# Identity products on TensorE ahead of the waits of three kinds of attention in a float32 model of one core

## The reference

```
first block: q, k normed, 8 query heads, 2 key heads, width 64
  s = q k' / 8 over the block itself, the one before it and 16 meta tokens, masked
  p = softmax([s, sink]);  out = p v                  # 5 blocks of 128, beside s5_ssm(...)
mixer A: score = sum_h w_h relu(iq_h ik');  keep the best 256 keys
         p = softmax(q k' / 8 + bias, kept keys only);  out = p v     # 4 heads of 64
mixer D: p = softmax(q k' / sqrt(96), causal);          out = p v     # 4 heads, keys of 96
```

## Time and profile before

| | |
|---|---|
| median of three runs | 4370.68 us |
| profiled execution | 4363.53 us |
| its span | 4362.3 us |
| TensorE busy | 4140.0 us, 19325 records |
| VectorE busy | 2287.6 us |
| ScalarE busy | 1407.6 us |
| mean granted clock | 0.956 |

### The profile page before, as it was taken

The page is one execution under the profiler, slowest core; times in us unless marked ns, Lnnn a source line. Parts: engine busy times, 40 slices in busy tenths (PEclk is TensorE's granted clock), DMA queues, the critical chain, the costliest instruction groups (busy, mean ns, idle before and its releaser), DMA issues.

```text
span 4362.3 us, 47791 instructions
## 1 busy us (share of the span) xinstructions
PE 4140.0 (95%) x19325; PEld 3249.6 (74%) x19325; DVE 2287.6 (52%) x3714; ACT 1407.6 (32%) x2385; POOL 192.0 (4%) x350
## 2 busy tenths in 40 slices
PE   8889999999999999999999978999999999789999
PEld 7767887666678888888878765787878787557877
DVE  5748887777734444444333776433243248754331
ACT  3444322333333333333222432422232233333221
POOL 8400000000000000000000010000000000100000
PEclk9779999999999999999999987999999999779999
DMA  3012444555566666662332210233323322003332
GB/s 114 11 39 86 125 138 127 182 185 178 175 195 197 190 188 189 189 189 85 93 96 73 82 46 1 78 92 97 97 78 96 97 73 78 27 1 97 92 97 73
DMA packets 253340, 473.59 MB, mean 109 GB/s; under 512 B 15856, under 2 KB 138896, under 8 KB 250944
## 3 DMA queue, kind: packets, MB, share of 16 engines
q1 hardware_dynamic: 253024, 470.45, 35.4%
q10 hardware_dynamic: 96, 0.08, 0.0%
HBM read 399.96 MB, written 70.52 MB: 108 GB/s over the span
## 4 chain that ended last, share of the span: by engine, by line
PE 79%; DVE 9%; ACT 3%; issue 1%; DMA 0%; POOL 0%; DVEq 0%; ACTq 0%; POOLq 0%; SPq 0%
PE ps L354 24%; PE ps L356 24%; PE ps L355 24%; DVE arena L2048 2%; PE ps L536 1%; DVE arena L2937 1%; DVE st L2935 1%; DVE arena L2044 1%; DVE arena L2045 1%; PE ps L1897 1%; PE ps L2425 1%; PE ps L2397 1%; ACT arena L1945 1%; DVE wlast L345 1%; PE ps L2400 1%
## 5 line engine op out<-in xcount | busy, mean ns | idle before, releaser
L345 DVE TENSOR_TENSOR wlast<-wraw,wlast 128x1024 fp32r<-128x1024 f32 x406 | 495.8, 1225 | 764.5 <-ACT wlast L335 764.2
L354 PE MATMUL ps<-XH,wlast 128*128 128x512 f32 (+1 forms) x1904 | 785.6, 413 | 0.0
L356 PE MATMUL ps<-XH,wlast 128*128 128x512 f32 (+1 forms) x1904 | 753.7, 396 | 0.0
L355 PE MATMUL ps<-XL,wlast 128*128 128x512 f32 (+1 forms) x1904 | 752.7, 395 | 0.0
L335 ACT ACTIVATE wlast<-wraw 128x1024 fp32r<-128x1024 f32 x406 | 426.8, 1056 | 407.6 <-PE ps L356 388.1
L345 DVE TENSOR_TENSOR wtwo<-wraw,wtwo 128x1024 fp32r<-128x1024 f32 x212 | 261.1, 1232 | 444.3 <-ACT wtwo L335 443.8
L356 PEld LDWEIGHTS ps<-XH,wlast 128*128 128x128 f32 x1904 | 360.3, 189 | 87.4
L354 PEld LDWEIGHTS ps<-XH,wlast 128*128 128x128 f32 x1904 | 361.3, 190 | 76.0 <-issue 5.0
L355 PEld LDWEIGHTS ps<-XL,wlast 128*128 128x128 f32 x1904 | 361.7, 190 | 70.9
L354 PE MATMUL ps<-XH,wtwo 128*128 128x512 f32 (+1 forms) x944 | 387.3, 410 | 0.0
L355 PE MATMUL ps<-XL,wtwo 128*128 128x512 f32 (+1 forms) x944 | 372.0, 394 | 0.0
(11 more groups left out here) (476 smaller groups left out, 6825.7 us busy)
## 6 DMA issues: line engine op xcount, KB each, us to landing
wraw<-in_ut SPq DMA_DIRECT2D x128, 512.0 KB, 4.2
wraw<-in_v SPq DMA_DIRECT2D x128, 512.0 KB, 3.9
wraw<-in_ffn_gate SPq DMA_DIRECT2D x88, 512.0 KB, 3.5
wraw<-in_ffn_up SPq DMA_DIRECT2D x88, 512.0 KB, 3.5
wraw<-in_ffn_down SPq DMA_DIRECT2D x88, 512.0 KB, 3.5
acts<-arena SPq DMA_DIRECT2D x128, 256.0 KB, 4.5
gates<-arena SPq DMA_DIRECT2D x16, 2048.0 KB, 9.0
arena<-gates SPq DMA_DIRECT2D x32, 1024.0 KB, 8.2
```

What stands on the lines that cost most here:

```text
L345: ve.e.tensor_tensor(W.items[n][8], W.rawof(n), W.items[n][7], ALU.subtract).then_inc(*ve.up("wlo", n))
L354: mm(out, lh, rh, start=start, stop=False)
L355: mm(out, lh, rl, start=False, stop=False)
L356: return mm(out, ll, rh, start=False, stop=stop)
```

## The change

A helper `busy(o, n)` is added to `Kernel`. It issues n matmuls of the 128 by 128 identity with itself, float32, into the first 128 columns of a bank, with start and stop set; the result is overwritten later or never read. It is called at three places:

- in `turn` of the first block's attention, 8 for head 0 and 2 for each other head. `open` has moved ahead of the wait for `se`, and the identity products stand between them;
- in its `value`, 2 for each head, in columns 256 to 383 of the result's bank, ahead of the wait for `PT`;
- in `turn` of the mixers' attentions, 3 for each head, between `open` and the wait for `ex`.

```diff
+    def busy(self, o, n):
+        for _ in range(n):
+            self.pe.e.matmul(o[:, 0:128], self.ident[:, :], self.ident[:, :], start=True, stop=True)
...
             def turn(hq):
+                o = k.open(3, 4, "pT", n, hq)
+                k.busy(o, 2 if hq else 8)
                 pe.wait_ge(*at("se", n))
-                o = k.open(3, 4, "pT", n, hq)
                 for kb in self.blocks(i):
...
             def value(h):
                 pv = k.open(4, 5, "pv", n) if h == 0 else k.got("pv", n)
+                k.busy(pv[:, 256:384], 2)
                 pe.wait_ge(*at("PT", n, h))
...
         def turn(n, h):
             o = k.open(b + 2, b + 3, id, "t", n, h)
+            k.busy(o, 3)
             pe.wait_ge(*at("ex", id, n, h))
```

## The result

The changed kernel takes 4388.16 us, the median of six runs (4387.67 to 4394.58). The kernel before took 4375.09 us beside it (six runs, 4369.83 to 4382.39). The ratio is 1.0032 with a 95% interval of [1.0019, 1.0045]: slower by a third of a per cent. Its profiled execution took 4388.0 us with a span of 4386.8 us, which is 24.5 us more than the span before. The mean granted clock rose from 0.956 to 0.968. So the clock did what the identity products were to do, and the kernel still lost. (The kernel before spread over 30 us in 80 runs, with a median of 4368.3 us; against that one the change costs 20 us.)

What follows compares the result with a forecast made beforehand. TensorE, VectorE, then TensorE were taken to bound the first attention; VectorE's search, then TensorE, each mixer. 4363.5 us + 19 (first attention) + 12 (two mixers) gave 4394.5, and 7.2 to the median gave 4402 us, range 4358 to 4435.

Steps and rivals of the forecast that it cites:

- The products fill no wait: At the attentions' transposes: products come after the bank's wait, fill next to nothing, and can pay only through the clock.
- 0.22 us a product at full clock: Price of one identity product on TensorE: 0.22 us at full clock, 0.43 at half; all 368 are 81 or 158 us.
- First attention to 153 us, +9.6: From 112 us, where TensorE sets the pace: 54 products, first 8 at half clock, 3.9 us gained; net +9.6 us.
- 153 to 199.4 us, +3: First attention's middle stretch, where VectorE sets the pace: 66 products, 14.5 us, mostly covered by VectorE's long products; +3 us.
- 199.4 to 246 us, +6.8: First attention's last stretch, where TensorE sets the pace: 56 products, 9.7 us gained from the clock; net +6.8 us.
- VectorE's search in the mixer: Each mixer to 2673 us: VectorE's search for the best keys fills 73.2 of 79 us and leads the chain.
- A mixer to 2673 us, +1: Mixer's first part: 45 products, 10 to 19 us, with VectorE as cover; +1 us, ends -3 and +3.
- A mixer's second part, +5: From 2673 to 2738 us: 51 products, nothing to hide under; +5 us, between +4.3 if the clock returns early and +13.7.
- The offset to the median, 7.2 us: Whole kernel: the profiled execution lies 7.2 us under the median of the runs, so 4394.5 us became 4402.
- The first rival: Full clock throughout: products hold the clock full in both attention stages, kernel faster by 10 us, 4361 us; chance 0.12.
- No response of the clock: Rival: half-clock stretches stay; +47 us for the first attention, +33 for the mixers, 4451 us; chance 0.10.
- hidden products: Rival: TensorE's idle time in the first attention's three stretches and the clock gain take the products up, 4371 us; chance 0.10.

Runs made afterwards that it cites:

- e7_double: The changed kernel with every count of identity products doubled (16, 4, 4 and 6; 736 in all); 4444.09 us, ratio 1.0174.
- e3_thin: The changed kernel with its 368 products using only 32 rows of the identity instead of 128, same columns; 4583.1 us, ratio 1.0527.
- e5_eight_only: The changed kernel with only the 8 products ahead of head 0 in the first attention kept, 64 in all; 4359.4 us, ratio 0.9982.
- e8_select: The kernel before plus 98 products at selected places in the first block and ahead of each mixer's first state product, score banks opened early; 4350.29 us, ratio 0.9958.
- e9_state_only: The kernel before plus only 20 identity products ahead of part B's first state product in each mixer, 40 in all; 4353.87 us, ratio 0.9982.

## Why the prediction was right

The direction held, and 4388 us lie inside the range around 4402. The size held less well: I had +31 us, and it is +13 us by the medians beside each other, +20 against all runs of the kernel before, and +24.5 in the profiles. The steps, one by one:

- *The products fill no wait.* Right. Transposes wait for nothing behind them, the bank's waits stand ahead of the products, and doubling the products costs 37 of 38.7 us (`e7_double`).
- *0.22 us a product at full clock.* Right: 1.79 us for eight. Nearly all 352 records of the first attention run at full clock.
- *First attention to 153 us, +9.6.* Right: +9.4 at that instruction on TensorE, +7.1 on VectorE. Only the first eight products at half, as assumed, and here they took 2.6 us instead of 3.4, since the clock returned among them.
- *153 to 199.4 us, +3.* Too small. On TensorE it is +7.4, for 14.5 us of products. VectorE's own steps in it are only 2.4 us later, so its long products did cover them, until 215 us; then it waited 8.95 us for TensorE where it had waited 1.91, and the offset was +17.7 at 206 us. The cover put the loss off and did not take it up. (My 3.8 us for the clock were 3.1: TensorE was busy 6.2 us at half clock there.)
- *199.4 to 246 us, +6.8.* Too large. On TensorE it is -0.9: the clock rose to 0.93, over the 0.75 that I had named, and gave back the whole price of 56 products. That the sum of the attention came out near (+16.1 for +19) is luck: these two terms were wrong in opposite ways by 4.4 and 7.7 us.
- *VectorE's search in the mixer.* I read 73.2 us as the search. That is all of VectorE's busy time in the stretch; lines 2935 and 2937 are 14.5 and 14.4 us of it. The term that hung on it, VectorE as the cover, came out near all the same.
- *A mixer to 2673 us, +1.* +2.1 and +1.4.
- *A mixer's second part, +5.* Too large: +1.5 and +1.6. The offset falls by 5.3 us at 2699, since the clock is back at 2693.8 us, where before, shifted by 15.7 us, it would have been 2712.5; then it rises by 6.8 to 2739 with the products at full clock. So the dense products did bring the clock back before the long scores, which is the nearer of my two ends (+4.3) and a bit beyond it. All four mixers that have these products show such a fall, by 4.7 to 5.3 us; so do two of the six without any product.
- *Between the mixers' stretches.* Not in my sum: another +2.5 us behind the first mixer's attentions and +0.7 behind the second's. The clock falls there at other times than before. `e5_eight_only`, without a product in the mixers, has +2.7 behind the first one as well, so I can't call these effects of the change. From 2390 us to the end the offset rises by 10.3 us, for a forecast of +12.
- *The offset to the median, 7.2 us.* This step failed. I took the distance of one profiled execution of the kernel before from the median of three runs and added it. After has 4388.0 in its profile and 4388.16 as its median. The 7.2 us were the chance place of one execution in a spread of 30 us. Without this term the sum says 4394.5. In the profiles the change costs +24.5, for +31 in my sum.
- *The first rival's price.* TensorE is busy 61 of 65 us in a mixer's second part, so full clock would give back 11.0 us there and not 11.7. The rival is 1 or 2 us dearer by that, which changes nothing.

The rivals: full clock throughout got its clock (1.00 and 0.93 in the last two stretches of the first attention, 0.96 in the mixer's second part), but the price of the products is larger than the clock returned; I had this rival at -10 us and the change is at +13 by the medians. Its ends for the attention were +2.4, 0 and -5.2, and TensorE's are +9.4, +7.4 and -0.9. No response of the clock is ruled out by `e3_thin` beside the change, and hidden products by `e7_double` and by the offsets of +16.1 and +14.7 behind the first attention.

What the Trainium skill advises (TensorE: Matmul & The Clock Gate, "Why this matters for your kernels"), to keep TensorE busy so that its clock stays up, held where the products were dense in rows, and the clock did stay up. It did not hold for the thin products, where TensorE was busy 106.2 of 108.5 us at 0.50. And a clock that stays up was not a faster kernel: the 176 products of the first attention bought it for 16 us.

Open: what decides where the clock falls. It is down from 111 to 152 us in `e8_select` and `e9_state_only` and only until 140 or 141 us in the two profiles of the kernel before, with the same TensorE work ahead. Whether less than 20 products, or transposes, in the wait of part B would do as well was not tried. Nor was it tried why the 8 products ahead of the state-space model's output bring nothing, nor why kernels with products in the first attention spread less.

## What to carry to other kernels

Work that keeps TensorE's clock up is free only where the engine would wait anyway: put it ahead of the wait, size it below the wait, and choose the wait that stands before the long half-clock stretch. Behind a wait that is over it costs its whole time. Whether the clock gives back more than that hangs on the dose: here not with 368 products (+0.32%), and by a little, as measured, with 64 of them (-0.18%) or with 368 transposes (-0.27%). Look in the trace at which of several waits is the real one, since an addition between two waits fills only the second; here the bank was the first, and the second was always over. Follow the loss on the engine that does the added work: another engine can run ahead on its own work for a while and show it late. Before a measured distance between one profile and a median goes into a sum, compare it with the spread of the runs.

## What I had not expected of the hardware

- 32-row products at the same columns hold the clock down: 0.50 over 108.5 us with TensorE busy 106.2 of them. 128-row products at the same places gave 1.00 and 0.93 in the last two stretches.
- Transposes of the identity at about 0.11 us (eight from 142.92 to 143.80 us) go far to hold it too: 0.87 and 0.84 against 1.00 and 0.93 with products at 0.22 in the last two stretches of the first attention, where the kernel before had 0.91 and 0.57.
- The same program gets its clock back at different points: at 3857.9 or 3871.0 us, which is 4.7 us of time, and runs spread over 0.7%. The kernels with full-row work in every unit of the first attention spread over 0.26% at most.
- 20 products in a wait of 7.35 us, 6.1 us of work, turned 65 us at 0.82 into 55 us at 1.00.
